# Moving the operands of an fp32r matmul kernel by 32 to 384 bytes within SBUF, with no instruction changed

## The reference

```python
for l in range(DEPTH):                                     # DEPTH = 2
    shift, scale, gate = adaln(c, w_ada_mix[l], b_ada_mix[l])   # c @ w + b, split in 3
    u = x * (1.0 + scale) + shift
    y = hybrid_mixer(u, w_in[l], ...)     # one input projection; GLU + 31-tap causal conv + LN + SiLU
                                          # beside sliding-window attention with sinks; then @ w_out
    x = layer_norm(DN_ALPHA * x + (1.0 + gate) * y, ln1_g[l], ln1_b[l])
    shift, scale, gate = adaln(c, w_ada_ffn[l], b_ada_ffn[l])
    u = x * (1.0 + scale) + shift
    val, g = jnp.split(u @ w_up[l], 2, axis=-1)             # 1024 -> 2 x 2816
    y = (val * silu(causal_dwconv(g, w3, b3))) @ w_down[l]  # 3 taps, 2816 -> 1024
    x = layer_norm(DN_ALPHA * x + (1.0 + gate) * y, ln2_g[l], ln2_b[l])
```

## Time and profile before

| | |
|---|---|
| median of the runs | 2143.56 us |
| the profiled execution's own time | 2145.49 us |
| its span, first to last instruction | 2143.7 us |
| TensorE busy | 97% of the span, 9499 matmuls |
| weight loads (PEld) | 80% |
| DVE / ACT / POOL busy | 55% / 48% / 65% |
| mean granted TensorE clock | 0.993 of full speed |
| DMA | 250.05 MB, mean 117 GB/s |

### The profile page before, as it was taken

The page is one execution under the profiler, slowest core; times in us unless marked ns, Lnnn a source line. Parts: engine busy times, 40 slices in busy tenths (PEclk is TensorE's granted clock), DMA queues, the critical chain, the costliest instruction groups (busy, mean ns, idle before and its releaser), DMA issues.

```text
span 2143.7 us, 27095 instructions
## 1 busy us (share of the span) xinstructions
PE 2089.0 (97%) x9499; PEld 1708.1 (80%) x9499; DVE 1179.0 (55%) x1898; ACT 1033.6 (48%) x1872; POOL 1403.5 (65%) x1769
## 2 busy tenths in 40 slices
PE   6999999999999999999999999999999999999996
PEld 5787778787888788888788888888778888888885
DVE  5698878666414554877532545587651454333224
ACT  3575356554515675364633656235552464333332
POOL 5987667765667887875557885564546776545553
PEclk9999999999999999999999999999999999999998
DMA  7644544533434354553233333432323232434332
GB/s 261 177 129 149 156 122 136 161 109 99 123 113 127 92 157 137 153 152 100 73 100 101 110 106 88 107 97 76 92 79 105 87 102 82 125 98 128 91 94 72
DMA packets 422165, 250.05 MB, mean 117 GB/s; under 512 B 49062, under 2 KB 393998, under 8 KB 422030
## 3 DMA queue, kind: packets, MB, share of 16 engines
q1 hardware_dynamic: 421162, 248.03, 39.1%
q10 hardware_dynamic: 867, 0.29, 0.1%
HBM read 242.71 MB, written 4.26 MB: 115 GB/s over the span
## 4 chain that ended last, share of the span: by engine, by line
PE 81%; DVE 6%; POOL 6%; ACT 3%; issue 2%; DMA 1%; SPq 1%; DVEq 0%; ACTq 0%; POOLq 0%
PE fg L807 26%; PE fg L809 25%; PE fg L808 25%; POOL w_lo L1722 3%; DVE bank_c L1393 1%; POOL ada_acc L1793 1%; PE bank_s L885 1%; ACT ada L1177 1%; DVE first_acc L1323 1%; DVE ada_acc L1438 1%; PE bank_t L907 1%; DMA stage_in<-in_x_dram 1%; PE bank_l L824 1%; ACT w_hi L1027 1%; PE bank_t L894 0%
## 5 line engine op out<-in xcount | busy, mean ns | idle before, releaser
L1722 POOL TENSOR_TENSOR w_lo<-raw,w_hi 128x256 fp32r<-128x256 f32 (+1 forms) x1440 | 1036.4, 750 | 671.1 <-ACT w_hi L1027 670.1
L807 PE MATMUL fg<-u_hi,w_hi 128*128 128x512 f32 x2112 | 844.5, 400 | 10.8 <-POOL w_lo L1722 4.4
L809 PE MATMUL fg<-u_hi,w_lo 128*128 128x512 f32 x2112 | 826.5, 391 | 0.0
L808 PE MATMUL fg<-u_lo,w_hi 128*128 128x512 f32 x2112 | 826.0, 391 | 0.0
L1027 ACT ACTIVATE w_hi<-raw 128x1024 fp32r<-128x1024 f32 (+2 forms) x392 | 379.4, 968 | 416.0 <-PE fg L809 322.4
L807 PEld LDWEIGHTS fg<-u_hi,w_hi 128*128 128x128 f32 x2112 | 398.6, 189 | 109.6 <-issue 20.9
L808 PEld LDWEIGHTS fg<-u_lo,w_hi 128*128 128x128 f32 x2112 | 398.8, 189 | 85.3 <-issue 5.3
L809 PEld LDWEIGHTS fg<-u_hi,w_lo 128*128 128x128 f32 x2112 | 398.5, 189 | 85.4
L1644 DVE SCALAR_TENSOR_TENSOR x<-fg,mod,x 128x512 f32<-128x512 f32 x160 | 120.0, 750 | 342.0 <-PE fg L809 341.7
L1393 DVE SCALAR_TENSOR_TENSOR bank_c<-glu,par,bank_c 128x512 f32<-128x512 f32 x448 | 305.8, 748 | 0.1
L807 PE MATMUL fg<-h_hi,w_hi 128*128 128x512 f32 x704 | 278.4, 395 | 0.0
(11 more groups left out here) (240 smaller groups left out, 1782.0 us busy)
## 6 DMA issues: line engine op xcount, KB each, us to landing
raw<-in_w_up_dram SPq DMA_DIRECT2D x176, 512.0 KB, 3.8
ada<-in_w_ada_ffn_dram SPq DMA_DIRECT2D x48, 512.0 KB, 4.6
raw<-in_w_down_dram SPq DMA_DIRECT2D x64, 384.0 KB, 3.4
raw<-in_w_in_dram SPq DMA_DIRECT2D x40, 512.0 KB, 3.9
raw<-in_w_down_dram SPq DMA_DIRECT2D x64, 320.0 KB, 3.0
ada<-in_w_ada_mix_dram SPq DMA_DIRECT2D x32, 512.0 KB, 4.7
raw<-in_w_in_dram SPq DMA_DIRECT2D x32, 256.0 KB, 3.8
raw<-in_w_out_dram SPq DMA_DIRECT2D x32, 256.0 KB, 2.9
```

Source lines behind the costliest of these rows:

```text
L807: pe.matmul(out[:], hi[:, k, :], rhi, start=k == order[0], stop=False)
L808: pe.matmul(out[:], hi[:, k, :], rlo, start=False, stop=False)
L809: ins = pe.matmul(out[:], lo[:, k, :], rhi, start=False, stop=k == order[-1])
L1722: ins = pool.tensor_tensor(w_lo[n % NRAW][:, ks, :], raw[n % NRAW][:, ks, :], w_hi[n % NHI][:, ks, :].bitcast(F32), ALU.subtract)
```

## The change

`sb` no longer adds the `_rest` tensors. Instead, four tensors that nothing uses are put in: 384 bytes ahead of `u_hi`, 32 ahead of `glu`, 32 ahead of `conv`, and 96 ahead of `stage_in` and `h_hi`. `small` (96 bytes) is allocated behind `const` instead of ahead of it. The instructions, their order, their waits and the semaphores are the same on every engine; only the addresses in them differ, and since the file has a few more lines, the line numbers (L807 becomes L812).

```diff
         def sb(name, shape, dt=F32, stack=ctx):
-            t = stack.enter_context(nc.sbuf_tensor(name, shape, dt))
-            if -(-int(np.prod(shape[1:])) // HALF_LINE) % 2:
-                stack.enter_context(nc.sbuf_tensor(name + "_rest", [P, HALF_LINE], F32))
-            return t
+            return stack.enter_context(nc.sbuf_tensor(name, shape, dt))
+
+        def unused(where, n):
+            sb(f"unused_{where}", [P, n * HALF_LINE])
...
         x = sb("x", [P, DT, SEQ])
+        unused("u", 12)
         u_hi, u_lo = [sb("u_hi0", [P, DT, T], F32R)], [sb("u_lo0", [P, DT, T], F32R)]
...
         diag = sb("diag", [P, TB, P])
-        small = sb("small", [P, 2, 3, TB])
         const = sb("const", [P, 2 * P + 2])
...
+        small = sb("small", [P, 2, 3, TB])
         par1 = sb("par1", [P, DEPTH, N1])
...
+        unused("glu", 1)
...
         glu = sb("glu", [P, CT, HIST + T])
+        unused("conv", 1)
...
         tanh_c = sb("tanh_c", [P, T])
+        unused("h", 3)
         with ExitStack() as region:
             stage_in = [sb(f"stage_in{i}", [P, D], stack=region) for i in range(4)]
...
```

## The result

The changed kernel takes 2148.98 us (median of 9 runs, 2146.93 to 2152.07), the kernel before 2143.52 (9 runs, 2142.19 to 2144.37). The ratio is 1.0028, with the interval 1.002 to 1.0036: slower by 5.5 us. The forecast was 2138.6, and the time lies outside its range, above.

What follows compares the result with a forecast made beforehand. TensorE bounds the kernel: number of matmuls times distance between starts. Gains of 4.7 (h) and 0.3 (start), others 0, sum to 5.0 us: 2145.49 to 2140.5 profiled, 2138.6 for runs; own range 2137 to 2140, 8-in-10 range 2134 to 2145.

Steps and rivals of the forecast that it cites:

- The step that failed: 2112 matmuls on h, moved to 128 mod 512, take u's distance between starts, 2.2 ns less each: 4.7 us gained.
- Rival A: Nothing changes: h's extra 2.2 ns comes from its region or its distance to the stationary tile; 2142.6 to 2143.9 us, chance 0.30.
- u and w at nothing: Matmuls on u: moving u and the weights from 128 to 0 mod 512 changes 0 us, ends -28 and +14.
- B: Matmuls on u get faster too at 0 mod 512, two steps of 2.2 ns for 6336 matmuls: 2111 us, chance 0.10.
- the 13.5 ns above the columns: Gap on u between 226.8 ns per matmul and the columns' 213.3, possibly alignment cost or the exchange of the weights.
- C: Matmuls on u (L807 to L809) get slower at 0 mod 512, 2.2 ns for 6336 matmuls: 2153 us, chance 0.08.
- DVE and ACT at nothing: New places of tanh_c, glu and gate cost 0 us; at most 33 ns an instruction on DVE, covered by its idle time.
- POOL: Its operands at 0 mod 512 change 0 us, bounds -0.5 and +0.5, from 0.8% of w_lo's 69 us on the chain.
- The start: In the first 31 us, with DMA engines full, better aligned weight and x transfers gain 0.3 us, bounds 0 and 1.2.
- The step from the profile to the runs: The profiled execution, 2145.49 us, lies 1.9 above the runs' median, 2143.56, so 1.9 comes off the predicted 2140.5.

Runs made afterwards that it cites:

- all at 0: The changed kernel with gate ahead of glu and no unused bytes ahead of glu and h, so u, weights and h begin at 0 mod 512: 2136.37 us.
- all at 256: The kernel before with 128 unused bytes ahead of u_hi and 192 ahead of stage_in, so u, weights and h begin at 256 mod 512: 2137.01 us.
- h alone at 128: The kernel before with 192 unused bytes ahead of stage_in, moving h from 448 to 128 mod 512, u and weights staying at 128: 2137.77 us.

## Why the prediction was wrong

**The step that failed** is h's: "I take 4.7, since u's row is the nearest: it has the very place that h gets". The measured sign is the other one: 2112 products at +3.8 ns, 8.0 us in the profile, where the sum had -4.7. The row was not the nearest in what counts. u's row had w at the same remainder; h after the change doesn't, since the same change took w from 128 to 0. The list of what is equal between h and u named "the same weight buffers", and that is the fault: the same buffer, but not the same distance to it. Rival A held the right quantity in one clause and even its numbers (320 before, 128 after), then priced it as "h keeps a distance" and so at nothing. It should have been priced from both sides, for a distance that costs 2.2 ns at 320 has no known price at 128. Two steps of 2.2 ns either way, 9.3 us, would have made the range 2134 to 2153, which holds the 2149 measured.

**u and w at nothing** was right: 226.7 to 226.8 ns, as both move together. The reason given was partly wrong. That loads from `ssum` and from `squares` have the same median looks at the load's duration beside a short product and never at the distance of starts of dense products; it says nothing on a stationary operand's place beside the moving one: moving u and w under an unmoved h costs 6.5 us.

**B** (u faster at 0) is out, and with it the guess that the 13.5 ns above the columns hold a cost of alignment: no place that was tried gave less than 226.7. **C** had the sign, and even looked at where moving rows and stationary rows lie together, but put the cost on u and ran the wrong way: equal remainders are the good case.

**DVE and ACT at nothing** was right: 748 and 755 ns with `glu` and `gate` elsewhere. **POOL** within its bounds, 752 for 750 ns. **The start**: 0.3 taken. The first products on the chain came 1.0 us earlier, as the bound of 1.2 allows, but in this trace only 0.2 of it reached the slabs; between the medians of two kernels with equal distances it may be 1.4. The rate rose from 343 to 365 GB/s. **The step from the profile to the runs**, 1.9 us taken off: the trace before holds the wait of 2.2 us near 264 us that only one other of the thirteen traces has, so it was right to take it off.

The rule of the Trainium skill, in "DMA: Bandwidth & Descriptors", section "How a descriptor splits into AXI transactions", on starts at multiples of 256, could not be weighed before. Now the runs bear on it: 366 and 367 GB/s with all targets of the start's large transfers at multiples of 256 (all at 0, all at 256), 365 in the changed kernel, where the tiles of x and one of the eight `first_ada` buffers are at 128, and 343 to 345 with these targets off such multiples (the kernel before, h alone at 128). That is 6% apart. Its beats for 2048-byte runs, 68 against 64, give 6% as an estimate, and the runs agree.

The Trainium skill has a rule for the other effect also, and there the runs differ. "TensorE: Matmul & The Clock Gate", section "Step-by-step: what each phase is for", gives TensorE two independent read ports and says: "Loading the next tile's weights doesn't steal SBUF read bandwidth from the running matmul." By it the place of w beside u would cost nothing. Measured: 226.7 ns for u in the kernel before against 233.3 with `w_hi` 128 bytes on, u and `w_lo` where they were. The runs show this dependence on the distance and not what makes it.

## What to carry to other kernels

In a dense stream of matmuls with a weight load each, put the moving and the stationary operand at the same remainder modulo 256, and check it again after any edit of the allocations: here a wrong pair costs up to 2.9% of each product (233.3 against 226.7 ns). Where the DMA engines are full, put their targets at multiples of 256 (366 against 345 GB/s here). Before a difference between two tensors in one trace is put down to a property of one of them, list in how many ways the two pairs differ, and give each way a price in the changed kernel.

## What was not expected of the hardware

- The time of an fp32r product of 512 columns with its load depends on the distance of its two operands: 226.7 ns at 0 modulo 256, 229 at 64, 232.4 to 233.3 at 128, 233.3 at 32, 192 and 224. At the full clock of 2.4 GHz the worst is 6.6 ns or 16 cycles more. 64 and 192 are not alike, so the sign of the distance counts. Why is open.
- One stationary operand out of place in three slows two of three intervals, and two in three slow all.
- DMA targets at multiples of 256 gave 22 to 24 GB/s more (343 to 365 and 367) with the DMA engines full.
- Behind the same wait of TensorE of some 2 us (2.02 and 2.12) the granted clock fell to 0.50 in one trace and stayed at 1.00 in another with the same instructions: 1.6 us, a quarter of the difference looked for here.
